# One layer of an RWKV-7, retention and mixture-of-experts step: inner levels of the chunk inverse as full-array matmuls, and the key norm with tokens on partitions

## What is computed

```python
kk = k * hp(k_k)
kk = kk / jnp.maximum(jnp.sqrt(jnp.sum(kk * kk, axis=-1, keepdims=True)), 1e-12)
...
def _wkv_step(S, inp):
    r, w, k, v, kk, b = inp
    sa = jnp.einsum('bhvk,bhk->bhv', S, -kk)
    S = S * w[:, :, None, :] + sa[..., :, None] * b[:, :, None, :] + v[..., :, None] * k[:, :, None, :]
    y = jnp.einsum('bhvk,bhk->bhv', S, r)
```

## Time and profile before

| | |
|---|---|
| Median of 3 runs | 1875.71 us (1875.41 to 1878.2) |
| Profiled execution | 1879.94 us, of which the span is 1878.2 us |
| PE busy | 1542.3 us (82%), 8870 matmul instructions |
| PEld busy | 880.0 us (47%) |
| DVE busy | 648.0 us (35%) |
| ACT busy | 304.9 us (16%) |
| POOL busy | 63.6 us (3%) |
| DMA | 510.35 MB, mean 272 GB/s |
| L723 (projection) | 1792 matmuls, 536.6 us busy, 437 ns each |

### The profile page before, as it was taken

One profiled execution on the slowest core, in us unless ns is written; L12 is line 12 of the kernel. 1 busy time (PEld: TensorE's weight loads), 2 busy tenths in 40 slices (PEclk: granted clock), 3 DMA queues, 4 the chain that ended last, 5 costly groups with the idle time before them and its releaser, 6 DMA issues.

```text
span 1878.2 us, 24556 instructions
## 1 busy us (share of the span) xinstructions
PE 1542.3 (82%) x8870; PEld 880.0 (47%) x8870; DVE 648.0 (35%) x1288; ACT 304.9 (16%) x704; POOL 63.6 (3%) x103
## 2 busy tenths in 40 slices
PE   7999999999999999999996675666757667576574
PEld 4676767676767676767752231222312223122121
DVE  6746565656565656410121120111201112010013
ACT  2323232323232323100112000000000000000012
POOL 1101010101010101000000000000000000000000
PEclk9999999999999999999997887888878888788787
DMA  7323232323232323374589999999999999999995
GB/s 286 109 100 113 92 120 82 120 82 120 82 120 82 120 82 120 110 292 165 204 373 426 429 426 429 429 428 428 429 428 427 429 429 429 427 429 430 428 403 212
DMA packets 71904, 510.35 MB, mean 272 GB/s; under 512 B 20496, under 2 KB 23696, under 8 KB 37808
## 3 DMA queue, kind: packets, MB, share of 16 engines
q1 hardware_dynamic: 71808, 509.60, 67.2%
q0 software_dynamic: 48, 0.12, 0.0%
HBM read 499.87 MB, written 9.82 MB: 271 GB/s over the span
## 4 chain that ended last, share of the span: by engine, by line
PE 41%; DMA 34%; DVE 16%; issue 4%; ACT 2%; SPq 1%; DVEq 1%; ACTq 0%
DMA arena<-w_up 22%; DVE arena L1424 16%; DMA arena<-w_down 12%; PE ps_PJ L723 11%; PE ps_C L1069 8%; PE ps_PJ L923 7%; ACT arena L1152 2%; SPq L560 1%; PE ps_C L1120 1%; PE ps_SB L1120 1%; PE ps_YB L1120 1%; PE ps_RT L1120 1%; PE ps_C L696 0%; PE ps_PJ L1023 0%; PE ps_SB L852 0%
## 5 line engine op out<-in xcount | busy, mean ns | idle before, releaser
L723 PE MATMUL ps_PJ<-arena 128*128 128x320 f32 x1792 | 536.6, 437 | 0.0
L1069 PE MATMUL ps_C<-arena 128*32 128x512 f32 x2048 | 285.1, 719 | 178.4 <-DMA arena<-w_gate 110.3
L723 PEld LDWEIGHTS ps_PJ<-arena 128*128 128x128 f32 x1792 | 324.7, 190 | 124.6 <-issue 17.9
L1424 DVE TENSOR_TENSOR arena<-arena,ps_PJ 128x512 f32<-128x512 f32 (+2 forms) x112 | 73.5, 657 | 614.7 <-PE ps_PJ L1023 495.3
L1069 PEld LDWEIGHTS ps_C<-arena 128*32 128x32 f32 x2048 | 79.3, 130 | 377.4 <-issue 375.0
L1152 ACT ACTIVATE arena<-arena 32x160 f32<-32x160 f32 (+9 forms) x350 | 146.6, 419 | 322.0 <-DVEq L422 134.7
L1424 DVE TENSOR_TENSOR arena<-arena 128x512 f32<-128x512 f32 (+12 forms) x311 | 161.8, 520 | 73.5 <-ACTq L422 41.2
L1152 ACT ACTIVATE arena<-ps_C 128x128 f32<-128x128 f32 (+3 forms) x68 | 27.4, 403 | 893.2 <-PE ps_C L1069 530.7
L923 PE MATMUL ps_PJ<-arena 128*128 128x320 f32 x512 | 142.4, 433 | 1.0 <-DVEq L422 1.0
L923 PEld LDWEIGHTS ps_PJ<-arena 128*128 128x128 f32 x512 | 95.5, 190 | 40.2 <-issue 3.3
L1424 DVE TENSOR_TENSOR arena<-ps_PJ,arena 128x512 f32<-128x512 f32 x32 | 22.1, 692 | 258.0 <-PE ps_PJ L1016 257.9
(11 more groups left out here) (181 smaller groups left out, 1175.7 us busy)
## 6 DMA issues: line engine op xcount, KB each, us to landing
arena<-w_down SPq DMA_DIRECT2D x64, 2048.0 KB, 21.5
arena<-w_gate SPq DMA_DIRECT2D x61, 2048.0 KB, 20.4
arena<-w_up SPq DMA_DIRECT2D x61, 2048.0 KB, 20.1
arena<-win SPq DMA_DIRECT2D x59, 1024.0 KB, 4.8
arena<-w_out SPq DMA_DIRECT2D x16, 1024.0 KB, 7.0
arena<-w_gate SPq DMA_DIRECT2D x6, 1024.0 KB, 8.0
arena<-xT SPq DMA_DIRECT2D x8, 640.0 KB, 7.4
arena<-s_ret SPq DMA_DIRECT2D x8, 512.0 KB, 3.8
```

The lines of the kernel that those rows point to most:

```text
L723: last = mm(pj(j)[:, 0:T], wt[j % NSLOT][:, kt, :], hT[:, kt, :], start=kt == 0, stop=kt == KT - 1)
L1069: last = mm((GB, UB)[u][h * CAP:(h + 1) * CAP, :], xg[:, kt, h * CAP:(h + 1) * CAP], w[h](k), start=kt == 0, stop=kt == KT - 1)
L1424: ins = build(*args)
```

## The change

In the key norm, the squares become the weights and two columns of `hsum` move: the sums land with tokens on partitions, as 3 groups of tokens by 2 heads, six columns (tokens 0 to 127, 128 to 255 and 192 to 319). Clamp, root and reciprocal work on these six (`rs6`). DVE then copies each of them over 64 columns (`rsx`, 128x384), and a new PE step `nb` multiplies it by columns of the unit matrix, which brings the factors back with channels on partitions, in PSUM, where DVE reads them for `kn`.

In the inverse, levels 1 to 4 lose the transposes `k1` to `k4` with their ACT copies, and POOL's four masks. `i1`..`i4` and `j1`..`j4` are four matmuls each with full 128x128 block-diagonal weights (`Ad`, made once in `u0`; `Ud`) and 32 moving columns. The level's mask is applied as DVE reads the result of `i` (`Zp`); after `j` DVE adds, transposes and spreads (not for the last). In `PLAN`, `ss` goes ahead of `b1k`, `rqb` behind `i3`, `xv` behind `j3`. In pair 0's table builder (`mk`) one transpose becomes a shorter one and a copy. The diff, lines of context cut:

```diff
     "C1": ["g1", "j1", "j2", "j3", "j4", "j5", "a0", "a1", "a2", "a3"],
-    "C2": ["g2", "k1", "k2", "k3", "k4", "k5", "s0", "s1", "s2", "s3"],
-    "SB": ["zw", "za", "ss", "g4", "zs1", "ds1", "zs2", "ds2", "rs0", "rs1", "bs", "gg", "as", "us"],
+    "C2": ["g2", "k5", "s0", "s1", "s2", "s3"],
+    "SB": ["zw", "za", "ss", "nb", "g4", "zs1", "ds1", "zs2", "ds2", "rs0", "rs1", "bs", "gg", "as", "us"],
...
 TT_ = [(0, P), (P, P), (TP, NS * TS)]
+NORM_AT = (0, P, T - P)
...
     "k": "-@g -u1 -th | -s1 | zw -u2 | -r2 -mr za | pc | -a2 pe | -mg | -s2",
-    "r": "@k ck | -r3 | sq p1 | -a3 b1k ss | b1l | ps -s3 | pk | b1 b2a",
+    "r": "@k ck | -r3 | sq p1 | -a3 ss b1k | b1l | ps -s3 nb | pk | b1 b2a",
     "v": "@r b2b cr -e3 | | | -my | g4 p2 | -mu g0 | g1 | g2 g3",
-    "q": "@v ax am -va u0 | cv us0 | | k1 i1 | zs1 xb | j1 pd | ds1 | k2 i2",
-    "kr": "@q | rqa j2 zs2 xk | | rqb k3 i3 | ds2 xv | j3 | | k4 i4",
+    "q": "@v ax am -va u0 | cv us0 | | i1 | zs1 xb | j1 pd | ds1 | i2",
+    "kr": "@q | rqa j2 zs2 xk | | i3 rqb | ds2 | j3 xv | | i4",
...
     "k": "| | | | | | | zw",
-    "r": "@k za sq pc ck lo | pe | | ss p1 b1k b1l | ps pk b1 b2a | | |",
+    "r": "@k za sq pc ck lo | pe | | ss p1 b1k b1l | ps nb pk b1 b2a | | |",
...
-        Zd = inv[:, 0:512].rearrange("p (b c j) -> p b c j", b=NB32, c=NC)
+        Ad = inv[:, 0:512].rearrange("p (c b j) -> p c b j", c=NC, b=NB32)
         Z5 = cut(512, 64, c=2)
-        Am = inv[:, 640:1152].rearrange("p (k c j) -> p k c j", k=INNER - 1, c=NC)
+        rs6 = cut(640, 6)
+        rsx = inv[:, 704:1088].rearrange("p (t f) -> p t f", t=3)
...
         V = cut(2560, NCH * P, c=NCH)
-        V2 = cut(3200, 128, c=NB32)
+        Zp = cut(3200, 128, c=NC)
...
         vchain, achain, pchain = sem("vector_chain"), sem("scalar_chain"), sem("pool_chain")
+        NINV = 2 * INNER + 1
...
                 if s == "ss":
                     wait_done(pe, "kk2", p)
-                    mm(b[:, 0:T], hsum, t2, start=True, stop=True).then_inc(full(s), 1)
+                    for t, t0 in enumerate(NORM_AT):
+                        last = mm(b[:, 2 * t:2 * t + 2], t2[:, t0:t0 + P], hsum[:, 0:P:HD], start=True, stop=True)
+                    last.then_inc(full(s), 1)
+                elif s == "nb":
+                    pe.wait_ge(done("rs"), 2 * p + 2)
+                    for t, t0 in enumerate(NORM_AT):
+                        new = t * P - t0
+                        last = mm(b[:, t * P:t0 + P], rsx[:, t, :], ident[:, new:P], start=True, stop=True)
+                    last.then_inc(full(s), 1)
...
                 elif s in ("zs1", "zs2"):
                     k = int(s[-1])
-                    pe.wait_ge(lmk, (INNER + 1) * p + k)
+                    pe.wait_ge(lmk, 2 * p + k)
...
                     if s == "ds2":
...
                     mm(b[:, 0:P], V[:, NC, :], Zs, start=True, stop=True).then_inc(full(s), 1)
-                elif s[0] == "k":
-                    pe.wait_ge(inverse, 2 * (INNER * p + int(s[1])) - 1)
+                elif s == "k5":
+                    pe.wait_ge(inverse, NINV * p + 2 * INNER)
                     nc.tensor.transpose(b[:, 0:P], Uc[:, :, :], ident).then_inc(full(s), 1)
+                elif s == "i5":
+                    pe.wait_ge(inverse, NINV * p + 2 * INNER + 1)
+                    pe.wait_ge(done("ac"), 2 * p + 2)
+                    for c in range(NC):
+                        last = mm(b[quarter[c], 0:HD], A5[:, c, :], Ud[:, c, 0:NB32:2, :], start=True, stop=True)
+                    last.then_inc(full(s), 1)
                 elif s[0] == "i":
-                    k = int(s[1])
-                    pe.wait_ge(inverse, 2 * (INNER * p + k))
-                    if k < INNER:
-                        pe.wait_ge(lmk, (INNER + 1) * p + 2 + k)
-                    else:
-                        pe.wait_ge(done("ac"), 2 * p + 2)
+                    pe.wait_ge(inverse, NINV * p + 2 * int(s[1]))
                     for c in range(NC):
-                        o = b[quarter[c], 0:P] if k < INNER else b[quarter[c], 0:HD]
-                        last = mm(o, Am[:, k - 1, c, :] if k < INNER else A5[:, c, :],
-                                  Ud[:, c, :, :] if k < INNER else Ud[:, c, 0:NB32:2, :], start=True, stop=True)
+                        last = mm(b[:, c * BK:(c + 1) * BK], Ad[:, c, :, :], Uc[:, c, :], start=True, stop=True)
+                    last.then_inc(full(s), 1)
+                elif s == "j5":
+                    wait_freed(pe, "i5", p)
+                    wait_freed(pe, "k5", p)
+                    for h in range(2):
+                        last = mm(b[quarter[2 * h], 0:P], Z5[:, h, :], V2d[:, h, :, :], start=True, stop=True)
...
                 elif s[0] == "j":
-                    k = s[1]
-                    wait_freed(pe, "i" + k, p)
-                    wait_freed(pe, "k" + k, p)
-                    if int(k) < INNER:
-                        for q in range(NB32):
-                            last = mm(b[quarter[q], 0:P], V2[:, q, :], Zd[:, q, :, :], start=True, stop=True)
-                    else:
-                        for h in range(2):
-                            last = mm(b[quarter[2 * h], 0:P], Z5[:, h, :], V2d[:, h, :, :], start=True, stop=True)
+                    wait_freed(pe, "i" + s[1], p)
+                    pe.wait_ge(inverse, NINV * p + 2 * int(s[1]) + 1)
+                    for c in range(NC):
+                        last = mm(b[:, c * BK:(c + 1) * BK], Ud[:, c, :, :], Zp[:, c, :], start=True, stop=True)
...
                 elif s == "ss":
                     wait_freed(act, s, p)
-                    A(rs, rs, ACT.Sqrt).then_inc(done("rs"), 1)
+                    A(rs6, rs6, ACT.Sqrt).then_inc(done("rs"), 1)
...
                     last.then_inc(done("ac"), 1)
-                elif s in ("k1", "k2", "k3", "k4"):
-                    wait_filled(act, s, p)
-                    A(V2[:, :, :], bank(s)[:, 0:P].rearrange("p (b j) -> p b j", b=NB32), ACT.Copy).then_inc(free(s), 1)
...
                 elif s == "ss":
                     wait_filled(dve, s, p)
-                    TSC(rs, bank(s)[:, 0:T], 1e-24, None, ALU.max).then_inc(free(s), 1)
+                    TSC(rs6, bank(s)[:, 0:6], 1e-24, None, ALU.max).then_inc(free(s), 1)
...
                 elif s == "ps":
...
-                    wait_done(dve, "rs", p)
-                    RECIP(rs, rs)
-                    STT(kn, xm["k"], scol(p, "k_k"), rs, ALU.mult, ALU.mult).then_inc(done("kn"), 1)
+                    dve.wait_ge(done("rs"), 2 * p + 1)
+                    RECIP(rs6, rs6)
+                    CP(rsx.rearrange("p t (h j) -> p (t h) j", h=2), rs6[:, :, None].broadcast_to([P, 6, HD])).then_inc(done("rs"), 1)
+                elif s == "nb":
+                    wait_filled(dve, s, p)
+                    STT(kn, xm["k"], scol(p, "k_k"), bank(s)[:, 0:T], ALU.mult, ALU.mult).then_inc(free(s), 1).then_inc(done("kn"), 1)
...
                         RED(folded[:, k, :], whole(lvl[k]), AX_X, ALU.add)
-                    TR(packed[:, 0:INNER, :].rearrange("p k j -> p (k j)"), folded[:, 0:INNER, :].rearrange("p k j -> p (k j)"))
+                    TR(packed[:, 0, :], folded[:, 0, :])
+                    CP(packed[:, 1:INNER, :], folded[:, 1:INNER, :])
...
                 elif s == "u0":
                     dve.wait_ge(done("ac"), 2 * p + 1)
+                    spread(Ad, Ac).then_inc(inverse, 1)
...
                     TR(Uc.rearrange("p c j -> p (c j)"), Vc.rearrange("p c j -> p (c j)")).then_inc(inverse, 1)
-                    spread(Ud, Uc).then_inc(inverse, 1)
+                    spread(Ud, Vc).then_inc(inverse, 1)
...
                 elif s in ("i1", "i2", "i3", "i4"):
                     wait_filled(dve, s, p)
-                    spread(Zd, bank(s)[:, 0:P].rearrange("p (b j) -> p b j", b=NB32)).then_inc(free(s), 1)
+                    TT(Zp[:, :, :], bank(s)[:, 0:P].rearrange("p (c j) -> p c j", c=NC),
+                       inner[int(s[1])][:, None, :].broadcast_to([P, NC, BK]), ALU.mult).then_inc(free(s), 1)
                 elif s in ("j1", "j2", "j3", "j4"):
...
                     TT(Uc[:, :, :], Uc[:, :, :], bank(s)[:, 0:P].rearrange("p (c j) -> p c j", c=NC), ALU.add).then_inc(free(s), 1).then_inc(inverse, 1)
-                    spread(Ud, Uc).then_inc(inverse, 1)
+                    if s == "j4":
+                        spread(Ud, Uc).then_inc(inverse, 1)
+                        return
+                    TR(Vc.rearrange("p c j -> p (c j)"), Uc.rearrange("p c j -> p (c j)"))
+                    spread(Ud, Vc).then_inc(inverse, 1)
...
                         TT(As[:, k - 1, :], GM[:, NC, 0:P], lvlT[k], ALU.mult).then_inc(lmk, 1)
-                    pool.wait_ge(done("ac"), 2 * p + 1)
-                    for k in range(1, INNER):
-                        TT(Am[:, k - 1, :, :], Ac[:, :, :], inner[k][:, None, :].broadcast_to([P, NC, BK]), ALU.mult).then_inc(lmk, 1)
```

## The result

The changed kernel takes 1893.04 us (median of 6 runs, 1890.05 to 1894.53) against 1875.68 before (now the median of six): ratio 1.0089, 95% interval 1.0076 to 1.0102, 17.4 us slower. The forecast was 11.0 slower. The profiled execution took 1892.82, its span is 1890.6.

The account below looks back on a forecast made before the run. PE's queue was taken to bound the pairs: 7 pairs of 1.3 - 0.1 make 8.4, pair 0 adds 2.6, so +11.0 on the median 1875.71 gives 1886.7 us. Range 1882 to 1892 (chance 0.65), whole range 1878 to 1895.

Parts of the forecast that it names:

- whole range of 1878 to 1895: Total time: the wider range, leaving out the two faster rivals and half of rival 1; 1882 to 1892 had 0.65.
- What bounds the pairs: Pairs: PE's queue sets the time, busy 91.05 of 92.87 us; other engines matter only where PE waits for them.
- ACT's four copies ... go at no gain: Inverse: removing ACT's four copies and POOL's four masks gains nothing, both engines being idle most of a pair.
- A pass at 0.11: PE: a matmul pass with full 128x128 weights and few moving columns costs 0.11 us, bounds 0.08 and 0.115.
- Rivals 2, 3 and 4: Short passes: at 0.08, 1869.9 (chance 0.06); by columns alone, 1840.2 (0.02); at 0.095, no measurable difference, 1878.3 (0.12).
- Key norm, -0.1 a pair: Key norm on PE: passes add 0.78, vanishing waits at g4 and L856 give back 0.86; sum -0.1 us a pair.
- Inverse, +1.3 a pair: Inverse on PE: 7.04 for 64 passes, 0.1 edge and 0.1 wait added, 5.94 removed; +1.3 us a pair.
- i1 now stands behind one more spread ... I count 0.1. The others I put at none: Inverse: new PE waits for DVE, 0.1 us at i1 behind an added spread of 0.69, none at the other steps.
- the 5.94: Inverse, removed from PE per pair: transposes 0.80, narrow i and j groups 2.88, edges 1.0, waits 1.26; sum 5.94 us.
- Pair 0, +2.6: First pair: +0.6 from the norm, with g3's later wait of 1.05 gone, and 2.0 from the inverse; +2.6 us.
- wait of 3.2 at nb: Pair 0: PE reaches nb at 50.83 but DVE finishes at 53.8, so nb starts at 54.0, a new 3.2 us wait.
- Rival 1, the wait moves: Each pair: nb waits 0.5, i1 and one other inner step 0.3 each; +8.8 us, 1895.5; chance 0.15.

Follow-up runs that it names:

- wide ss: The changed kernel with ss moving all 128 columns of hsum through each of its three weights instead of two: 1891.9 us.
- norm alone: The kernel before with only the change's key norm (ss, nb, their order in tile r), the inverse as before: 1877.17 us, ratio 1.0002.
- both moves: The changed kernel with us0 behind g1 in tile v and pair 0's nb three parts later: 1885.4 us, ratio 1.0052.
- inverse alone: The changed kernel with the norm's edits taken back, keeping the change's inverse and its order in tiles q and kr: 1892.39 us, ratio 1.0086.

## Why the prediction was right or wrong

- **The number**: the direction was right and the size too small, 17.4 where 11.0 was forecast. 1893.04 lies outside the forecast's own 1882 to 1892 and inside the whole range of 1878 to 1895. What made the difference, the wait at zs1 and the clock in pair 0, were no terms of that range: it allowed for the price of a pass, a wait at nb, and 1.5 for pair 0.
- **What bounds the pairs**: right. Whatever the change took from DVE (1.7 a pair) and POOL came to nothing except where PE had waited. "ACT's four copies ... go at no gain" was too short: with the copies in place, moving xv as the change does left j4 waiting 0.75 for ACT.
- **A pass at 0.11**: right for full weights, 0.81 to 0.83 for eight and 0.08 at the edge behind, 0.89 to 0.91 against the forecast's 0.88. The wide ss shows it is not the columns. The floor of some 25 ns for 1 to 64 columns, which the Trainium skill (TensorE: Matmul & The Clock Gate, Back-to-back issue gap) gives for the isolated gap between matmuls, did not rule here: no pass with fresh 128x128 weights came near it. Rivals 2, 3 and 4 fall with this.
- **Key norm, -0.1 a pair**: right in kind; the norm alone showed -0.26. In steady pairs nb did meet DVE within 0.1 us and waited for nobody, and g4's and L856's waits went.
- **Inverse, +1.3 a pair**: here the step "i1 now stands behind one more spread ... I count 0.1. The others I put at none" failed. What stood behind the added spread in DVE's queue was not only i1 but us0, and zs1 on PE waits for us0: 0.65 a pair. I looked at the steps of the chain that was changed and not at the other chain queued behind it. Moving us0 gave 4.7 us back, 3.3 of them in the pairs of the trace. The rest of the sum held: with both moves a pair takes 93.82, with the norm alone 92.57, so the inverse without the wait costs 1.25, which is 7.2 less the 5.94. A steady pair came to +1.5 instead of +1.2: the wait, 0.5 net, was missed, and the norm gave back 0.2 more than forecast, which hid part of it.
- **Pair 0, +2.6**: measured +5.55. The wait of 3.2 at nb was forecast (3.0 came, nb at 54.0 as said), and that g3's wait would go. Missed was what the wait does to the clock: 5.4 us at 1.2 GHz, which make nb 0.66 and the 32 passes 2.17 longer, 2.8 together. That the rest comes out at 2.7, next to the forecast's 2.6, is partly luck. The norm alone moves k5 of pair 0 by 1.70, of which the clock makes 1.8, so nearly nothing without it where 0.6 was forecast; the inverse alone moves it by 2.8 where 2.0 was.
- **The sum**: pair 0 came out 2.95 over its forecast and the seven other pairs 1.7 (10.08 against 8.4), which makes 11.0 into 15.6, the shift of k5 in pair 7. The output projection adds 0.4. The remaining 1.4 between the medians would have to lie in the experts, where executions differ by more than that; what it is stays open.
- **Rival 1, the wait moves**: it did, but not to nb or i1 in every pair. It went to zs1, and to nb in pair 0 only.

## What to carry to other kernels

Where one engine's queue is full, count an edit by its instructions on that queue. On PE, while no more than 128 columns move, count passes with fresh weights and not columns: eight full-array passes cost 0.9 us where eight narrow ones side by side cost 0.36 and 0.1 at each edge. Work taken from other engines pays only for waits, and a wait may be had for free by order: list who waits, and what stands ahead in the awaited engine's queue, on every engine, and for every chain that shares it. Before work is put ahead of something in a queue, look for all who are queued behind it, and in a first iteration look out for idle time of the matmul engine, which is paid twice.

## What the runs showed of the hardware that was not expected

- An idle time of 3.0 us on PE was followed by 5.4 us at half clock, though PE was busy without a break from its end (changed kernel, pair 0). Idle times of 2.1 and 1.1 us in the earlier trace rows had no such effect, and with other work in its place the clock stayed at 1.00.
- What such an idle time costs on top of itself is not fixed: the clock fell while PE was still idle in the changed kernel, and only behind the idle time in the two others, and the cost was 2.8 us there and 1.8 in each of these (norm alone, wide ss). Each figure is from one execution.
- A copy of 384 columns within SBUF took 0.36 us, shorter than the 0.45 of a tensor_scalar with 320 columns beside it; I had counted 0.59 by the clamp's row, which reads PSUM.
- The reciprocal's time goes with its columns: 2.15 us for 320, 0.19 for 6.
- Six passes with 2 moving columns took 0.59, 0.098 each, a little under the 0.112 of those with 128; the projection behind them gave the difference back.
